# Gate-weight tiles behind the residual sums, keys two steps ahead and normalisation at other steps in a four-head scan

## What is computed

```python
# per head, direction and chunk (stabiliser terms left out)
s   = einsum('td,sd->ts', q, k) * exp(log_D - m_t)        # scores inside the chunk
num = s @ v + inter_w * (q @ C)                           # inside part + carried state
h   = num / max(|den|, exp(-m_t))
C   = decay * C + einsum('s,sd,se->de', ws, k, v)         # ws: the weight of a key
# per head, both directions summed
h   = (h - mean) * rsqrt(var + EPS)                       # over the head's 256 channels
out = h * mh_norm_w + skip_w * c                          # then times silu(m_z)
x   = x + concat(y_pool, out) @ w_out
gates = concat(q, k, v) @ w_gates + b_gates               # q, k, v are block-diagonal maps
```

## Time and profile before

| | |
|---|---|
| median of three runs | 1850.66 us |
| the profiled execution | 1852.29 us |
| its span, first to last instruction | 1850.5 us |
| TensorE (PE) busy | 1758.3 us, 95% |
| VectorE (DVE) busy | 1011.4 us, 55% |
| ScalarE (ACT) busy | 622.3 us, 34% |
| GpSimd (POOL) busy | 397.2 us, 21% |
| mean granted clock of TensorE | 0.984 of 2.4 GHz |

### The profile page before, as it was taken

One profiled execution on the slowest core, in us unless ns is written; L12 is line 12 of the kernel. 1 busy time (PEld: TensorE's weight loads), 2 busy tenths in 40 slices (PEclk: granted clock), 3 DMA queues, 4 the chain that ended last, 5 costly groups with the idle time before them and its releaser, 6 DMA issues.

```text
span 1850.5 us, 21024 instructions
## 1 busy us (share of the span) xinstructions
PE 1758.3 (95%) x8312; PEld 1423.7 (77%) x8312; DVE 1011.4 (55%) x1292; ACT 622.3 (34%) x802; POOL 397.2 (21%) x230
## 2 busy tenths in 40 slices
PE   7999999999999999998889999999999898889997
PEld 5888887887788888887768766777788777668885
DVE  5443243434667776667655665234563477797223
ACT  5110012234555665555511200000023756663002
POOL 3223232322201111100022322222233000003331
PEclk9999999999999999999989999999999999899998
DMA  5011130141010011110422211121123102145112
GB/s 202 35 69 69 46 137 35 57 159 35 24 35 10 26 35 35 35 35 12 182 86 91 80 34 35 63 74 47 57 86 130 58 24 91 46 152 201 46 34 91
DMA packets 38065, 129.46 MB, mean 70 GB/s; under 512 B 5220, under 2 KB 5604, under 8 KB 37712
## 3 DMA queue, kind: packets, MB, share of 16 engines
q1 hardware_dynamic: 37968, 128.12, 19.4%
HBM read 96.42 MB, written 31.56 MB: 69 GB/s over the span
## 4 chain that ended last, share of the span: by engine, by line
PE 76%; DVE 15%; ACT 6%; issue 1%; DMA 1%; SPq 0%; DVEq 0%; POOL 0%; ACTq 0%; POOLq 0%
PE pair L682 45%; PE pair L879 6%; PE pair L932 5%; PE aux L907 3%; PE pair L920 2%; DVE pt_lo L1610 2%; PE aux L1160 2%; PE aux L1042 1%; PE pair L1146 1%; PE pair L748 1%; DVE stat_b L1824 1%; ACT bm_b L1505 1%; DVE o_lo L1610 1%; PE aux L1013 1%; DVE prob L1831 1%
## 5 line engine op out<-in xcount | busy, mean ns | idle before, releaser
L636 POOL CAST w_hi<-w_raw 128x1024 fp32r<-128x1024 f32 x107 | 116.1, 1085 | 1286.1 <-issue 1285.2
L682 PE MATMUL pair<-op_hi,w_hi 128*128 128x512 f32 x992 | 313.0, 397 | 11.5 <-DVE op_lo L1615 11.5
L682 PE MATMUL pair<-op_lo,w_hi 128*128 128x512 f32 x992 | 306.6, 390 | 0.0
L682 PE MATMUL pair<-op_hi,w_lo 128*128 128x512 f32 x992 | 306.1, 390 | 0.0
L638 POOL TENSOR_TENSOR w_lo<-w_raw,w_hi 128x1024 fp32r<-128x1024 f32 x107 | 268.6, 2510 | 8.6
L682 PEld LDWEIGHTS pair<-op_hi,w_hi 128*128 128x128 f32 x992 | 185.6, 188 | 60.2 <-issue 21.6
L682 PEld LDWEIGHTS pair<-op_lo,w_hi 128*128 128x128 f32 x992 | 186.8, 188 | 39.3
L682 PEld LDWEIGHTS pair<-op_hi,w_lo 128*128 128x128 f32 x992 | 186.8, 188 | 39.1
L1610 DVE TENSOR_TENSOR pt_lo<-pair,pt_hi 128x1024 fp32r<-128x1024 f32 x64 | 78.4, 1225 | 93.0 <-ACT pt_hi L1367 91.1
L1367 ACT ACTIVATE pt_hi<-pair 128x1024 fp32r<-128x1024 f32 x64 | 65.8, 1028 | 163.2 <-PE pair L920 82.0
L879 PE MATMUL pair<-opb_hi,w_hi 128*128 128x512 f32 x256 | 100.7, 393 | 0.0
(11 more groups left out here) (338 smaller groups left out, 3074.3 us busy)
## 6 DMA issues: line engine op xcount, KB each, us to landing
w_raw<-weight_units SPq DMA_DIRECT2D x107, 512.0 KB, 3.4
xf<-y_dram SPq DMA_DIRECT2D x12, 512.0 KB, 4.5
xa<-x_t SPq DMA_DIRECT2D x8, 512.0 KB, 8.5
x_dram<-xa SPq DMA_DIRECT2D x8, 512.0 KB, 5.8
xc<-x_dram SPq DMA_DIRECT2D x8, 512.0 KB, 7.5
x_dram<-xc SPq DMA_DIRECT2D x8, 512.0 KB, 2.7
y_dram<-y_d SPq DMA_DIRECT2D x8, 512.0 KB, 2.7
mz_dram<-y_d SPq DMA_DIRECT2D x8, 512.0 KB, 2.9
```

The costliest lines, as they stand in the source:

```text
L636: pool.tensor_copy(w_hi[:, u % 2, :], w_raw[:, u % 3, :]).then_inc(w_hi_done, 1)
L682: mm = pe.matmul(acc[:, cols], w, x[:, kx, cols], start=(first and k == 0 and n == 0), stop=(last and k == KT - 1 and n == 2))
```

## The change

It touches four places.

- y2: vector builds 12 of the 24 `bdt` tiles behind residual 0 and 12 behind residual 1, and waits for the constants only there. The gate products move from behind unit 2 to behind unit 3.
- Rows: `load_bm(0)` no longer waits for `gt_ready`. Planes 8 to 11 of y3 are loaded before the store of head 2's planes instead of behind it.
- Scan: `k_w` has two buffers for each direction, and a key is weighed two steps ahead, behind the copy of the inside part. Statistics, factor, shift, normalisation, skip, transposes and gain of heads 0 and 1 are one step earlier or, for the statistics, in five steps instead of eight.
- End of the scan: the gates of head 2 and low parts 0 and 1 leave head 3's steps and follow the scan on vector, in a new order with the other parts; the last head's output planes have a buffer of their own (`out_last`, over the last two planes of `o_lo`); the third unit of y3 takes its high products first and then its low ones.

```diff
@@ tensors
+        k_w = keep("k_w", [P, 2, NDIR, MD])
-        k_w = keep("k_w", [P, NDIR, MD])
+        out_last = nc.alloc_sbuf_tensor_at("out_last", [P, 2, S], F32, offset=at[0] + 4 * S * (2 * KT - 2))
@@ tables
-        FACTOR_AT = [8] * LAST + [2]
-        LN_AT = [{9: (0, 1, 2, 3), 10: (4, 5, 6, 7)}] * LAST + [{4: (0, 1, 2), 5: (3, 4, 5), 6: (6, 7)}]
-        SKIP_AT = [(11, 12)] * LAST + [(6, 7)]
-        TURN_AT = [(12, 14)] * LAST + [(7, 9)]
-        SHIFT_AT = [9] * LAST + [3]
-        GAIN_AT = [(13, 15)] * LAST + [(8, 10)]
+        STATS_AT = {0: (0, 1), 1: (2,), 2: (3,), 3: (4, 5), 4: (6, 7)}
+        FACTOR_AT = [7] * LAST + [2]
+        LN_AT = [{8: (0, 1, 2), 9: (3, 4, 5), 10: (6, 7)}] * LAST + [{4: (0, 1, 2), 5: (3, 4, 5), 6: (6, 7)}]
+        SKIP_AT = [(10, 11)] * LAST + [(6, 7)]
+        TURN_AT = [(11, 13)] * LAST + [(7, 9)]
+        SHIFT_AT = [8] * LAST + [3]
+        GAIN_AT = [(12, 14)] * LAST + [(8, 10)]
@@ SP
-                    sp.wait_ge(gt_ready, 1)
                     load_bm(0)
             weights_to(BASE[5] + 4)
+            for k in range(KT, KT + 4):
+                load_y("y3", k, xf, KT)
             store_head(2)
-            for k in range(KT, THROUGH["y3"]):
+            for k in range(KT + 4, THROUGH["y3"]):
                 load_y("y3", k, xf, KT)
@@ TensorE
                 unit(BASE[3] + e, BASE[3] + e, opb_hi, opb_lo, "y2")
-                if e == 2:
+                if e == 3:
...
-                if 2 <= n < 2 * KT - 2:
-                    unit(BASE[5] + n, BASE[5] + e, o_hi, o_lo, "y3", kt0=KT * i, wait_operand=(n == 2),
+                if n == 2:
+                    pe.wait_ge(w_split, BASE[5] + n + 1)
+                    for k in range(KT):
+                        pe.wait_ge(hi_ready, OP0["y3"] + KT + k + 1)
+                        high_products(BASE[5] + n, k, o_hi, HI_SLOT[KT + k], pair[BASE[5] % 2], first=False)
+                    for k in range(KT):
+                        pe.wait_ge(op_ready, OP0["y3"] + KT + k + 1)
+                        mm = low_products(BASE[5] + n, k, o_lo, True, pair[BASE[5] % 2], kt0=KT)
+                    mm.then_inc(unit_done, 1)
+                elif 3 <= n < 2 * KT - 2:
@@ ScalarE
-                if ks >= 2:
-                    act.wait_ge(upd_done, ks - 1)
+                if ks >= 4:
+                    act.wait_ge(upd_done, ks - 3)
...
             weigh_keys(0, 0)
+            weigh_keys(0, 1)
             inside_copy(0, 0)
...
-                        if nm < NDIR * (CH - 1):
-                            weigh_keys(nh, nm)
                         inside_copy(nh, nm)
+                    kh, km = (h, m + 2) if m + 2 < NDIR * CH else (h + 1, m + 2 - NDIR * CH)
+                    if kh < MH and km < NDIR * (CH - 1):
+                        weigh_keys(kh, km)
@@ vector
-            dve.wait_ge(consts_d, 80)
-            for i in range(3 * KT):
-                block_diagonal(bdt[:, i, :], blocks_d[:, i % 3, i // 3, :], bmask_d, bdt_ready)
             for k in range(KT):
                 dve.wait_ge(x_loaded[k], 32)
                 add_residual(BASE[3], k, xc)
                 gained_low(k, xc, gain_both[:, k:k + 1], OP0["in"], op_hi, op_lo)
                 accumulate(2, k, sq_c, acc_c, acc_g)
+                if k < 2:
+                    dve.wait_ge(consts_d, 80)
+                    for i in range(12 * k, 12 * k + 12):
+                        block_diagonal(bdt[:, i, :], blocks_d[:, i % 3, i // 3, :], bmask_d, bdt_ready)
...
-                    if n == 6 and h == LAST:
-                        out_gate(h - 1, 1)
-                    if n in (2, 3) and h == LAST:
-                        y_low(n - 2)
-                    if n == 5 and h == LAST:
-                        out_gate(h - 1, 0)
             divide(MH - 1, CH - 1, 1)
-            for k in range(2, 4):
+            for k in range(4):
                 y_low(k)
-            norm_shift(MH - 1)
+            norm_shift(LAST)
             for k in range(4, 6):
                 y_low(k)
             dve.wait_ge(skip_ready, 2 * MH)
-            for k in range(6, 11):
+            for k in range(6, 8):
                 y_low(k)
+            for i in range(2):
+                out_gate(LAST - 1, i)
+            for k in range(8, 10):
+                y_low(k)
+            for i in range(2):
+                out_gain(LAST, i, aux[:, i * S:(i + 1) * S])
             dve.wait_ge(ln_done, MH)
-            y_low(11)
+            for k in range(10, 12):
+                y_low(k)
             for i in range(2):
-                out_gain(MH - 1, i, aux[:, i * S:(i + 1) * S])
-                y_low(12 + i)
-                out_gate(MH - 1, i)
-            for k in (14, 15):
+                out_gate(LAST, i)
+            for k in range(12, 16):
                 y_low(k)
```

More of the change, by code:

```diff
@@ L273, in build @@
         v_tok = keep("v_tok", [P, 2, CH, VE])
-        k_w = keep("k_w", [P, NDIR, MD])
+        at[0] += 4 * NDIR * MD
+        assert at[0] >= max(phase_start + 4 * S * 3 * KT, y_d_start + 4 * 2 * S)
         bm_b = keep("bm_b", [P, NDIR, S])
@@ L383, in back, with out_buffer @@
             return 16 * (before + k // KT + 1)
+        def out_buffer(h):
+            return out_e if h < LAST else out_last
         def side_bank(h, n):
@@ L685, in unit_tile, with high_products @@
                 return mm
-            def high_products(u, k, hi, slot, acc=None):
+            def high_products(u, k, hi, slot, acc=None, first=True):
                 acc = pair[u % 2] if acc is None else acc
@@ L693, in high_products, with low_products @@
                         pe.matmul(acc[:, cols], w[:, u % 2, k * P:(k + 1) * P], hi[:, slot, cols],
-                                  start=(k == 0 and w is w_hi), stop=False)
-            def low_products(u, k, lo, last, acc=None):
+                                  start=(first and k == 0 and w is w_hi), stop=False)
+            def low_products(u, k, lo, last, acc=None, kt0=0):
                 acc = pair[u % 2] if acc is None else acc
@@ L1159, in _ @@
                             o = aux[:, 2 * HALF + i * HALF:2 * HALF + i * HALF + VE]
-                            mm = pe.matmul(o, k_w[:, d, i * P:(i + 1) * P], v_tok[:, h % 2, c, :],
+                            mm = pe.matmul(o, k_w[:, ks // 2 % 2, d, i * P:(i + 1) * P], v_tok[:, h % 2, c, :],
                                            start=True, stop=True)
@@ L1191, in _ @@
             for n, (e, i) in enumerate(Y3_UNITS):
-                if 2 <= n < 2 * KT - 2:
-                    unit(BASE[5] + n, BASE[5] + e, o_hi, o_lo, "y3", kt0=KT * i, wait_operand=(n == 2),
+                if n == 2:
[8 more added lines that the diff above has]
+                elif 3 <= n < 2 * KT - 2:
+                    unit(BASE[5] + n, BASE[5] + e, o_hi, o_lo, "y3", kt0=KT * i,
                          first=(i == 0), last=(i == 1), slots=HI_SLOT)
@@ L1228, in y3_hi @@
             def y3_hi(k):
-                src = xf[:, k % KT, :] if k < 6 or KT <= k < THROUGH["y3"] else (bm_b if k < KT else out_e)[:, k % 2, :]
+                src = xf[:, k % KT, :] if k < 6 or KT <= k < THROUGH["y3"] else (bm_b if k < KT else out_last)[:, k % 2, :]
                 y_hi("y3", k, src, o_hi, HI_SLOT[k])
@@ L1489, in weigh_keys @@
                 c = n if d == 0 else CH - 1 - n
-                if ks >= 2:
-                    act.wait_ge(upd_done, ks - 1)
+                if ks >= 4:
+                    act.wait_ge(upd_done, ks - 3)
                 r = 16 + MH * d + h
-                link(act.activation(k_w[:, d, :], k_tok[:, h % 2, c, :], ACT.Copy, scale=g_tok[:, c, r:r + 1]),
+                link(act.activation(k_w[:, ks // 2 % 2, d, :], k_tok[:, h % 2, c, :], ACT.Copy, scale=g_tok[:, c, r:r + 1]),
                      kw_ready)
@@ L1535, in out_skip @@
                 n = 2 * h + i
-                if h >= 1:
+                if 1 <= h < LAST:
                     act.wait_ge(y_stored[i], stored("y3", KT + 2 * h - 2 + i))
-                link(act.activation(out_e[:, i, :], c_rows[:, n, :], ACT.Copy, scale=col("skip", n)), skip_ready)
+                if h == LAST:
+                    act.wait_ge(a_done, NDIR * CH * MH)
+                    act.wait_ge(upd_done, NDIR * (CH - 1) * MH)
+                link(act.activation(out_buffer(h)[:, i, :], c_rows[:, n, :], ACT.Copy, scale=col("skip", n)),
+                     skip_ready)
             for n in FIRST_PREP:
@@ L2128, in out_gain @@
                 dve.wait_ge(skip_ready, n + 1)
-                link(dve.scalar_tensor_tensor(out=out_e[:, i, :], in0=src, scalar=col("mh_norm", n),
-                                            in1=out_e[:, i, :], op0=ALU.mult, op1=ALU.add), ht_read)
+                out_i = out_buffer(h)[:, i, :]
+                link(dve.scalar_tensor_tensor(out=out_i, in0=src, scalar=col("mh_norm", n),
+                                            in1=out_i, op0=ALU.mult, op1=ALU.add), ht_read)
             def out_gate(h, i):
```

(8 more changed lines are left out.)

2 lines of the change are left out of this document (1 added, 1 removed).

## The result

The changed kernel takes 1838.22 us (median of 6 runs, 1833.94 to 1843.42) against 1851.09 us of the kernel before in the same comparison (6 runs): ratio 0.9933, 95% interval 0.9917 to 0.9949, so 12.4 us less in the means (12.9 in the medians). The forecast was 1830 in a range of 1821 to 1841: the sign and the range held, the gain was some 8 us short. The profiled execution took 1836.77 us (span 1835.0, mean granted clock 0.988), against 1852.29 (1850.5, 0.984) before; I had expected 1831.6 for it. Three more sets of runs of the kernel before bring its median to 1850.68 us (41 runs, 1848.07 to 1855.83).

What follows compares the result with a forecast made beforehand. TensorE is busy 95% of the span, so only its stalls and slow clock can be won. 11.5 + 14.5 - 2.3 - 3.0 = 20.7 us off 1852.29 gives 1831.6, or 1830 as a median; range 1821 to 1841.

Steps and rivals of the forecast that it cites:

- Part A: Layer y2: tiles behind residual sums 0 and 1, gate products one unit later; gain 11.5 us, bounds 8.5 and 12.
- Part B: Rows of head 0 loaded without the wait for `gt_ready`: gain 0, bounds 0 and 0.3 us.
- Part C: Scan: keys two steps ahead, normalisation one step earlier, last head relieved; scan ends 14.5 us earlier, bounds 6 and 17.
- rival 2: Short stalls swing the scan's clock, bringing back 8.4 us of heads 1 to 3 instead of 3; 1835.5, chance 0.18.
- my allowance: Scan: 3 us taken off for slow clock behind the new schedule's stalls, between 0 and 8.
- Head 3: Last head of the scan: vector loses two gates and two low parts, 5.0 us; 4.6 us won.
- The tail: Behind the scan, work moved out of it returns: -2.0 - 2.0 + 1.7 = -2.3 us.
- the term +1.7: Tail: the 1.8 us slow stretch at 1656 should go as the stalls in front of it shrink.
- The base: Whole kernel: gains taken from one profiled execution of 1852.29 us, 1.6 us above the median of 1850.66.
- Rival 3: Scan: vector's queue keeps its pace despite earlier keys; only y2's gain and some 1 us remain; 1838, chance 0.09.
- Rival 5: Slower: short stalls hold TensorE at 1.2 GHz in heads 1 to 3; 1859 with 65 us granted 0.5; chance 0.04.

Runs made afterwards that it cites:

- twin: Changed kernel with the load queue's wait for `gt_ready` put back: 1838.36 us (6 runs).
- fillers: Unread small products put ahead of TensorE's waits in heads 1 to 3: 1831.90 us on the changed kernel, 1849.66 us on the kernel before.
- The fillers in the tail: Changed kernel with unread products in the scan, 8 more in front of it and 10 ahead of the third unit's wait: 1834.71 us, ratio 0.9901.
- part A alone: Kernel before with only y2's tiles behind residual sums and gate products one unit later: 1843.28 us, again 1839.54 us; median over ten runs 1840.4.

## Why the prediction was right in kind and too large

**Part A: right.** 11.5 us were forecast, 11.6 are in the two chains and 11.4 in the means. The tiles took the 6.8 us that I had allowed for once (2.8 us lost beside GpSimd's split) both times, and both covers held, with less to spare than forecast: 4.5 us at residual 1 (5.6 expected), and 3.3 us at the gate products (952.4 to 955.65; 7 expected).

**Part B: right**, nothing.

**Part C, heads 0 to 2: right within the scatter, for a reason that I had only half.** I had 9.7 us for heads 1 and 2 (4.6 + 5.1) less 3 for the clock. M2-M3 fell by 5.35 us in the changed kernel's trace and by 7.25 in that of its twin; with the clock held full by fillers it is 9.15, near the 9.7. Of these 9.15, 3.1 are clock that the kernel before lost here and 6.1 the new schedule. So the queues were followed rightly, as far as these traces can tell, and the clock took back 1.9 to 3.8 us: rival 2 in kind, my allowance in size. What was late next was the state, as said: 1.22 us in head 1 and 1.90 in head 2 (1.2 and some 1.75 to 2 expected), and 3.83 at head 3's start (3.6 expected). The section of the Trainium skill that the prediction weighed ("TensorE: Matmul & The Clock Gate", "A second HAM failure mode: psum-queue depth-cycling") is borne out in kind here: waits of 1.1 to 1.9 us between groups of products were followed by granted clocks of 0.57 (1524 to 1528) and 0.50 (1576 to 1582) in the changed kernel, and with the waits of heads 1 to 3 filled it was 1.00.

**Head 3: the size failed.** 4.6 us were forecast for 5.0 us less of vector's work; M3-M4 fell by 2.4. (The three heads of the forecast, 4.6, 5.1 and 4.6, add up to 14.3 and not to the 14.5 of its sum.) The forecast counted from vector's first copy, and took head 3 as vector's throughout. From the first copy (1595.43) to the last division (1640.8), with its statistics to 1641.5, vector took 46 us and not 44. Behind its 3.83 us wait TensorE lost 1.6 us to the slow clock, and there vector waits in turn:

```profile
1595.43 0.69 DVE L2102 COPY state<-aux 128x514 f32<-128x514 f32 x1
...
1598.35 0.69 DVE L2102 COPY state<-aux 128x514 f32<-128x514 f32 x1 [1.03 <-PE aux L1169]
```

and between M3 and M4 it idled 6.4 of 38.6 us, where before it idled 3.9 of 40.7: with less work of its own it waits for TensorE's. With a full clock the removal of the same four operations is worth 3.3 us (40.69 to 37.40), still not 4.6.

**The tail: the term that was mis-sized most.** Forecast -2.3, measured -5.3 (195.12 to 200.42; -5.2 in the twin). The first pair's waits on low parts are listed with 1.6 us (2.0 expected), but they cost more: from the first low products of its second unit to the transposes behind them it is 6.06 us, and before it was 3.63, so 2.4 us are lost. After, then before:

```profile
1646.41 2.43 PE L710 MATMUL pair<-o_lo,w_hi 128*128 128x512 f32 x10
...
1652.47 1.91 PE L1190 MATMUL aux<-ident,h_tok 128*128 128x128 f32 x16
```

```profile
1668.83 3.79 PE L701 MATMUL pair<-o_lo,w_hi 128*128 128x512 f32 x16
1672.46 1.91 PE L1181 MATMUL aux<-ident,h_tok 128*128 128x128 f32 x16
```

The third unit's wait is 2.63 us (2.2 expected), and high part 15 holds it up by another 0.25:

```profile
1669.73 0.74 PE L702 MATMUL pair<-o_hi,w_hi 128*128 128x512 f32 x2 [2.63 <-ACT o_hi L1258]
...
1671.00 1.22 PE L702 MATMUL pair<-o_hi,w_hi 128*128 128x512 f32 x2
```

```profile
1667.28 2.49 DVE L2162 TENSOR_TENSOR out_last<-out_last,mz_sb 128x1024 f32<-128x1024 f32 x2
```

High part 14 waits for the last gates, which vector reaches only at 1667.28; vector's rows beside GpSimd's split took 5.2 us more than alone, and I had allowed 4.4. But behind this wait the clock falls (1.22 us for two products that take 0.62), another 1.7 us, and I had counted only what the tail would win from a slow stretch that goes, not that its own new wait brings one. The slow stretch at M4 did go (the clock is 1.00 for 30 us behind it), as forecast. From its last row before the wait (1666.48) the third unit takes 10.8 us to the next unit (1677.26); at the pace of its rows at full clock this is 5.9, so wait, high part 15 and slow clock cost 4.9 together. With the 2.4 of the first pair it is 7.3 us, where before had some 1.9 in the same part (0.2 of waiting, 1.7 of clock): 5.4, which is the whole of the 5.3 measured. So the step that failed most is the term +1.7, set down for a slow stretch that goes, when a new wait brought another of the same size. The fillers in the tail give back 1.2 us. Together with head 3 the relief of the last head is worth nothing: -3.3 and +3.5 between the two kernels that differ in it alone.

**The base: read from one trace.** The sum was made against an execution 1.6 us above the median and I took only these 1.6 us off. But part A alone, whose scan is that of before, has M2-M3 at 164.22 in one trace and 161.67 in another: the slow stretches that I read as the scan's own are there in some executions and shorter in others. From M1 to the end the two traces of before average 924.7 us, the two of the changed kernel (with and without the `gt_ready` wait) 908.8: 15.9 us less, while the medians are 12.5 apart. Both traces of before are above its median. The trace can't say how much each execution loses to the clock, and a range was the right place for it.

Of the rivals, 2 came nearest in its mechanism: the clock swings in the scan (1835.5). Rival 3 (the scan doesn't pay, 1838) gives the number but not the cause: the heads paid 5 to 7 us, head 3 and tail lost 3 together. Rival 5 has its mechanism too, but with some 13 us of the scan granted 0.5 (6.6 lost) and not 65: TensorE recovered after every wait.

## What to carry to other kernels

When work is moved off the last stage of a serial part, price the stage behind it with the same care, the clock behind its new wait included: here one head's relief of 5 us was worth nothing (+3.3 and -3.5 us). Where a wait of 1 to 4 us can't be removed, a few unread products ahead of it are worth trying, since here they kept the clock for what follows; in the changed kernel they brought 6 us, in the kernel before under 2. Size them from a row of the same shape and type, shorter than the wait. And read gains between kernels at marks of their own code, in more than one execution, before believing 2 us.

## What the runs showed of the hardware

The same waits don't always cost the same. Behind the gate products of y2 the slow stretch cost 1.7 us in one execution and near 3.4 in another of one kernel; behind three waits of 1.1 to 1.2 us it was there in one trace and absent in the next. Of the clock lost in the scan only a part was time lost: of some 8 us in before's heads 3.1 came back with fillers, of 6.6 in the changed kernel's 4.7 (2.8 against its second trace). TensorE's listed idle time understates a late operand: three waits of 0.5 us made a run of 16 products 2.4 us longer. And of vector's 128x128 tile products those that ran beside GpSimd's weight split took 1.0 to 2.4 us in place of 0.30; the one that began at 935.24 took 2.44 us and ended at 937.68, where GpSimd's subtraction (935.14, 2.39 us) had ended at 937.53.
